# Hybrid convolution and gated-attention block: a different head, and LayerNorm statistics one query block later

## The chip, the cores and the metric

The kernel runs on the eight cores of one Trainium2 chip. Each core computes 4096 of the 32768 tokens by itself, with no exchange between cores. The metric is the device time of the slowest core, in microseconds.

## The reference

x is (16, 2048, 1024) in float32; everything is causal.

```python
h = rms_norm(x, norm_g)
c_val, c_gate, c_z, q, k, v, g_lr, g_r, m_conv, m_gla = split(h @ w_in)
# conv branch
u = c_val * sigmoid(c_gate)
u = depthwise causal conv over 31 positions(u) + conv_b
u = silu(layer_norm(u)) * silu(c_z);   y_conv = u @ w_conv_out
# gated linear attention, 4 heads, key 128, value 256
log_a = log_sigmoid(g_lr @ gate_w2 + gate_b) / 16
S_t = diag(a_t) S_{t-1} + k_t^T v_t;   o_t = q_t S_t / sqrt(128)
y_gla = (rms_norm(o) * silu(g_r)) @ w_gla_out
y = sigmoid(m_conv) * y_conv + sigmoid(m_gla) * y_gla
out = rms_norm(x + y @ w_out, final_g)
```

## The kernel before

A core works through eight tiles of 512 tokens, tile 0 to tile 7. The weights are 88 blocks of 128x1024; a tile uses 96 units (the other eight, the convolution taps, are built in place by L339). Tiles 0 to 2 fetch most blocks in float32 (`sb_stg<-w`, 512 KB each, five staging slots), cast them to bf16 in turn on VectorE (L352) and ScalarE (L355), and a third of them per tile is written back in bf16 (`w_b<-sb_wn`). From tile 3 on all blocks are read back in bf16, with 22 slots. `units()` is called just ahead of the matmuls that use a block; it first casts up to four blocks beyond (`LOOK`), and the casts stand in the engines' queues at that point.

The order of the instructions on each engine is the order in which the program is written; `Sched` only adds the semaphore waits. Every engine takes its own instructions strictly in order, and all hardware DMAs are issued by SyncE (SP) in program order too. Only the 128 KB `gw2` is issued by GpSimd.

**The head.** SP issues the first 128 rows of x (`x0_load(0)`), the constants `cst` (identity, mask, gate weights, taps; 512 KB, in FP slots 0 and 1), the per-channel parameters `pp` (20 KB: 160 bytes in each of 128 rows), the norm gain `Gn` (512 KB, broadcast), the other three row blocks of x, and then the first five weight blocks. VectorE casts five parts of `cst` (L279 to L283), negates four columns of `pp` (L284), and clears `scanm`, `u` and `onesb` (L286 to L290). Then for each of the four row blocks: ScalarE squares x with an accumulated sum (L440), GpSimd makes the reciprocal root by a power with -0.5 read from `pp[:, 26:27]` (L443, L446), VectorE scales (L449), TensorE transposes into the one bank `pb6` (L458), and ScalarE copies to `hT` (L461). The order on ScalarE is square 0, square 1, copy 0, square 2, copy 1, square 3, copy 2, copy 3. The square's elementwise output goes to the `hb` slot (two of them) that L449 then overwrites.

**A tile.** GLU (units 0 to 15), values (16 to 23), convolution (24 to 31), eight query and key blocks (`qk`, h = 0 to 7, L409), the attention's silu gate (`wide_tm`, L645), then the attention with conv-gate and merge-gate blocks between its parts, the two output projections of the branches (L419), and the final projection (L795), among whose work the next tile's norm is prepared.

**The statistics.** After the convolution, the sum over channels and the sum of squares stand in `FP` slots 8 and 9, still spread over 128 partitions. `conv_split(0)` and `conv_split(1)` make a bf16 part and a remainder of each on VectorE (L527, L529), giving four pieces `HP`. `conv_stat` sums them over the partitions by four matmuls with a matrix of ones (L536) into banks 4 and 5. `conv_rstd` makes mean and reciprocal deviation (L541 to L546 on VectorE, L549 and L551 on ScalarE), and `ln(c)` normalises block c (L555 GpSimd, L558 VectorE, L561 ScalarE). VectorE also evicts each query and key block (L663, L667). The order around them:

```python
qk(t, h)
if h == 0: conv_split(1)
if h == 1: conv_stat()
if h == 2: conv_rstd()
if h >= 3: ln(h - 3)
```

The remaining three `ln` calls stand in the first gate half (`wide_tm(t, U_GR(0), ...)`), after each of its first three row blocks. The query and key blocks go to banks 2, 7, 0, 1, 3 in turn.

Of the kernel before, what the change touches and what calls it, by code (L numbers as in the profile page):

```python
# [148 lines left out]
def build_nc(n_tiles=NT):  # L149
# [16 lines left out]
    def newsem(name):  # L166
        dma_sem_names.append(name)
        return name

    with ExitStack() as es:  # L170
        def sb(name, shape, dt):
            return es.enter_context(nc.sbuf_tensor("sb_" + name, shape, dt))
# [55 lines left out]
        def mk(name, n=None):  # L228
            if n is None:
                B[name] = Buf(name)  # L230
            else:
                B[name] = [Buf("%s%d" % (name, i)) for i in range(n)]
# [27 lines left out]
                            d.r[kk] = vv  # L260

        B["cst"] = B["FP"][0]
        mk("taps"); mk("m32")

        def x0_load(s):
            S.op("sp", lambda e: e.dma_start(out=U1[:, 2 * s:2 * s + 2, :].rearrange("p a t -> p (a t)"),
                                             in_=x_d[s * 128:(s + 1) * 128, :]),
                 writes=B["U1"][2 * s:2 * s + 2], dma_sem=newsem("x0_%d" % s))

        x0_load(0)  # L270
        S.op("sp", lambda e: e.dma_start(out=cst, in_=cst_d), writes=[B["FP"][0], B["FP"][1]], dma_sem=newsem("c_cst"))
        S.op("sp", lambda e: e.dma_start(out=pp[:], in_=pp_d), writes=[B["pp"]], dma_sem=newsem("c_pp"))
        S.op("sp", lambda e: e.dma_start(out=Gn[:], in_=ng_d.partition_broadcast(128)), writes=[B["Gn"]],
             dma_sem=newsem("c_gn"))
        for s_ in range(1, 4):
            x0_load(s_)
        S.op("pool", lambda e: e.dma_start(out=gw2[:], in_=gw2_d), writes=[B["gw2"]], dma_sem=newsem("c_gw"))

        S.op("dve", lambda e: e.tensor_copy(out=identb[:], in_=cst[:, 0:128]), reads=[B["cst"]], writes=[B["identb"]])  # L279
# [1 line left out]
        S.op("dve", lambda e: e.tensor_copy(out=wglr[:], in_=cst[:, 256:512]), reads=[B["cst"]], writes=[B["wglr"]])  # L281
        S.op("dve", lambda e: e.tensor_copy(out=taps[:], in_=cst[:, 512:768]), reads=[B["FP"][1]], writes=[B["taps"]])
        S.op("dve", lambda e: e.tensor_copy(out=m32[:], in_=cst[:, 768:800]), reads=[B["FP"][1]], writes=[B["m32"]])  # L283
        S.op("dve", lambda e: e.tensor_scalar(out=pp[:, 32:36], in0=pp[:, 32:36], scalar1=-1.0, scalar2=0.0,  # L284
                                              op0=ALU.mult, op1=ALU.add), reads=[B["pp"]], writes=[B["pp"]])
        S.op("dve", lambda e: e.memset(scanm[:], 1.0), writes=[B["scanm"]])  # L286
        S.op("dve", lambda e: e.memset(scanm[:].rearrange("p (c t) -> p c t", c=4)[:, :, 0:1], 0.0),
             reads=[B["scanm"]], writes=[B["scanm"]])
        S.op("dve", lambda e: e.memset(u[:], 0.0), writes=B["u"])
        S.op("dve", lambda e: e.memset(onesb[:], 1.0), writes=[B["onesb"]])  # L290
# [142 lines left out]
        def pre_elem(t, s):  # L433
            p = s % 2
            if t == 0:
                xs, xbuf = U1[:, 2 * s:2 * s + 2, :].rearrange("p a t -> p (a t)"), B["U1"][2 * s:2 * s + 2]
            else:
                xs, xbuf = xa[:, p, :], [B["xa"][p]]
            col = (t * 4 + s) % 8
            S.op("act", lambda e, p=p, col=col: e.activation(  # L440
                out=hb[:, p, :], in_=xs, func=AF.Square, accum_out=ssx[:, col:col + 1]),
                reads=xbuf, writes=[B["hb"][p], B["ssx"][col]])
# [3 lines left out]
            S.op("pool", lambda e, col=col: e.tensor_tensor(  # L446
                out=ssx[:, col:col + 1], in0=ssx[:, col:col + 1], in1=pp[:, 26:27], op=ALU.pow),
                reads=[B["ssx"][col], B["pp"]], writes=[B["ssx"][col]])
# [323 lines left out]
        def fin(t, s):  # L772
            col = 8 + (t * 4 + s) % 8
            ub = B["U1"][2 * s:2 * s + 2]
            hv = HP[:, 0:2, :].rearrange("p a t -> p (a t)")
            S.op("act", lambda e: e.activation(out=hv, in_=u1v(s), func=AF.Square, accum_out=ssx[:, col:col + 1]),
                 reads=ub, writes=[B["HP"][0], B["HP"][1], B["ssx"][col]])
            S.op("pool", lambda e: e.tensor_scalar(
                out=ssx[:, col:col + 1], in0=ssx[:, col:col + 1], scalar1=1.0 / D, scalar2=EPS,
                op0=ALU.mult, op1=ALU.add), reads=[B["ssx"][col]], writes=[B["ssx"][col]])  # L780
            S.op("pool", lambda e: e.tensor_tensor(
                out=ssx[:, col:col + 1], in0=ssx[:, col:col + 1], in1=pp[:, 26:27], op=ALU.pow),
                reads=[B["ssx"][col], B["pp"]], writes=[B["ssx"][col]])
# [49 lines left out]
        def tile(t):  # L833
# [34 lines left out]
            for h in range(8):  # L868
                qk(t, h)
                if h == 0:  # L870
                    conv_split(1)
                if h == 1:
                    conv_stat()
                if h == 2:
                    conv_rstd()
                if h >= 3:
                    ln(h - 3)
            rbf(t, 0)
            set_pbanks([1, 3, 4, 5, 2, 7, 0])
            wide_tm(t, U_GR(0), sgr, B["sgr"], AF.Silu, False, lambda s: ln(5 + s) if s < 3 else None)  # L880
            wide_tm(t, U_GR(1), sgr, B["sgr"], AF.Silu, False)

            set_pbanks([5, 7])
# [186 lines left out]
```

How the kernel before makes its waits and increments, by code:

```python
    def replay(self, eng, engobj, eng_sems, dma_sems):  # L135
        for o in self.prog[eng]:
            for k, v in o.waits:
                if k[0] == "e":
                    engobj.wait_ge(eng_sems[k[1]], self.cnts[k[1]][v])
                else:
                    engobj.wait_ge(dma_sems[k[1]], v)
            if o.fn is None:
                continue
            inst = o.fn(engobj)
            if o.dma_sem is not None:
                inst.then_inc(dma_sems[o.dma_sem], 16)
            elif o.marked:
                inst.then_inc(eng_sems[eng], 1)
```

## Time and profile before

| | us |
|---|---|
| median of 3 runs | 1612.04 |
| lowest, highest | 1610.75, 1613.39 |
| the profiled execution's own time | 1609.87 |
| span of its slowest core (core 7) | 1608.3 |
| span of its fastest core (core 3) | 1592.6 |
| TensorE busy, core 7 | 1478.3 |

The span is the time from the first to the last instruction of a core; about 1.6 us of the execution lie around it. PE is the matrix engine, PEld its weight loads, DVE VectorE, ACT ScalarE, POOL GpSimd, SP the engine that issues the DMAs. In a timeline the columns are start in us, duration in us, engine, line, operation, output and inputs with shapes, the count, and in brackets the idle time before it and what released it.

### The profile page before, as it was taken

To read this page: it belongs to the slowest core of one execution; us is meant where nothing else is said; L and a number is where in the kernel's file an instruction comes from. 1 tells how busy PE (TensorE), PEld (TensorE's weight loads), DVE (VectorE), ACT (ScalarE), POOL (GpSimd) and SP (SyncE) were. 2 spreads that over 40 slices of the span, in tenths; PEclk is the share of its full clock that TensorE was granted. 3 is DMA by queue.
4 is the path that set the end of the run, shared out by engine and by line. 5 is a ranking of instruction groups with operands and counts; after the bars stand their busy time and mean duration, and the time that the engine had idled before them with its cause. 6 is when DMAs were issued, how large, how long until landed. Compare 5 with 4: busy or idle time off the path is not lost.

```text
span 1608.3 us, 28736 instructions; the slowest of 8 cores (1592.6 to 1608.3 us)
## 1 busy us (share of the span) xinstructions
PE 1478.3 (92%) x8960; PEld 703.2 (44%) x8960; DVE 890.8 (55%) x1259; ACT 705.4 (44%) x1184; POOL 555.2 (35%) x659
## 2 busy tenths in 40 slices
PE   4687989688999899999999999999999999999997
PEld 1233533234544345444554445444544445444553
DVE  3466645475545665476634665376644675366633
ACT  4235755226644256433644245233644246332631
POOL 1123223224223342254423452353423352352512
PEclk9898999889999999999999999999999999999999
DMA  6987899976899868898464955568564856568451
GB/s 184 292 235 222 274 314 318 291 231 200 269 322 286 255 205 252 268 268 243 153 220 143 247 177 184 177 192 242 151 223 145 229 188 200 178 180 241 134 175 53
DMA packets 174820, 352.29 MB, mean 219 GB/s; under 512 B 19536, under 2 KB 60624, under 8 KB 174672
## 3 DMA queue, kind: packets, MB, share of 16 engines
q1 hardware_dynamic: 174528, 350.32, 71.5%
q8 instruction: 76, 1.25, 0.3%
q14 instruction: 72, 0.59, 0.1%
q0 software_dynamic: 144, 0.13, 0.1%
HBM read 301.75 MB, written 48.76 MB: 218 GB/s over the span
## 4 chain that ended last, share of the span: by engine, by line
PE 73%; DMA 10%; DVE 7%; issue 4%; ACT 3%; SPq 2%; POOL 1%; DVEq 0%; POOLq 0%; ACTq 0%
PE ps_pb L409 33%; PE ps_pb L645 13%; PE ps_pb L419 11%; PE ps_pb L795 6%; PE ps_pb L507 4%; DMA sb_stg<-w 4%; DMA usc<-sb_u 3%; DVE sb_U L513 1%; DVE sb_FP L520 1%; SPq L498 1%; DMA w_b<-sb_wn 1%; ACT sb_wn L355 1%; PE ps_pb L707 1%; PE ps_pb L703 1%; PE ps_pb L712 1%
## 5 line engine op out<-in xcount | busy, mean ns | idle before, releaser
L409 PE MATMUL ps_pb<-sb_hT,sb_wn 128*128 128x512 bf16 x2152 | 492.7, 383 | 16.1 <-ACT sb_wn L355 6.9
L409 PEld LDWEIGHTS ps_pb<-sb_hT,sb_wn 128*128 128x128 bf16 x2152 | 209.8, 99 | 271.2 <-issue 38.2
L645 PE MATMUL ps_pb<-sb_wn,sb_hT 128*128 128x512 bf16 x768 | 191.6, 408 | 53.1 <-ACT sb_wn L355 33.1
L409 PE MATMUL ps_pb<-sb_hT,sb_stg 128*128 128x512 bf16 x920 | 207.0, 379 | 1.2 <-issue 0.8
L419 PE MATMUL ps_pb<-sb_big,sb_wn 128*128 128x512 bf16 x744 | 174.7, 382 | 0.4 <-DVE sb_wn L352 0.4
L936 POOL TENSOR_TENSOR sb_yb<-sb_FP 128x512 bf16<-128x512 f32 x64 | 82.7, 1293 | 213.0 <-DVE sb_FP L933 213.0
L645 PEld LDWEIGHTS ps_pb<-sb_wn,sb_hT 128*128 128x128 bf16 x768 | 77.6, 103 | 163.0 <-issue 87.0
L409 PEld LDWEIGHTS ps_pb<-sb_hT,sb_stg 128*128 128x128 bf16 x920 | 89.4, 98 | 105.4 <-issue 2.6
L355 ACT ACTIVATE sb_wn<-sb_stg 128x1024 bf16<-128x1024 f32 x88 | 92.3, 1050 | 98.3 <-DMA sb_stg<-w 98.1
L674 POOL TENSOR_SCALAR sb_Rbf<-sb_Tst,sb_gar 128x256 bf16<-128x256 f32 x128 | 65.7, 531 | 190.8 <-DVE sb_Tst L718 190.7
L522 POOL TENSOR_TENSOR sb_FP<-sb_FP,sb_yb 128x512 f32<-128x512 f32 x56 | 73.8, 1319 | 157.0 <-ACT sb_yb L516 157.0
L555 POOL TENSOR_TENSOR sb_U<-sb_U,sb_FP 128x512 f32<-128x512 f32 x64 | 97.1, 1544 | 57.3 <-DVE sb_FP L541 57.3
L419 PEld LDWEIGHTS ps_pb<-sb_big,sb_wn 128*128 128x128 bf16 x744 | 72.1, 99 | 83.7 <-issue 4.3
L352 DVE CAST sb_wn<-sb_stg 128x1024 bf16<-128x1024 f32 x89 | 68.5, 776 | 63.6 <-DMA sb_stg<-w 63.5
L926 ACT ACTIVATE sb_FP<-ps_pb 128x512 f32<-128x512 f32 x64 | 38.0, 594 | 137.0 <-PE ps_pb L409 116.9
L489 POOL COPY sb_halo<-sb_u 128x30 bf16<-128x30 bf16 x64 | 50.9, 796 | 127.4 <-DVE sb_u L486 127.4
L449 DVE SCALAR_TENSOR_TENSOR sb_hb<-sb_xa,sb_ssx,sb_Gn 128x1024 bf16<-128x1024 f32 x28 | 36.0, 1284 | 102.2 <-POOL sb_ssx L446 102.2
L481 ACT ACTIVATE sb_FP<-ps_pb 128x512 f32<-128x512 f32 x64 | 38.1, 595 | 121.2 <-PE ps_pb L409 80.1
L795 PE MATMUL ps_pb<-sb_wn,sb_yb 128*128 128x512 bf16 x384 | 86.5, 379 | 4.8 <-ACT sb_wn L355 1.8
L740 DVE SCALAR_TENSOR_TENSOR sb_big<-ps_pb,sb_sso,sb_sgr 128x256 bf16<-128x256 f32 x128 | 61.9, 483 | 45.5 <-POOL sb_sso L732 35.5
L507 PE MATMUL ps_pb<-sb_big,sb_wn 128*32 128x512 bf16 x1472 | 80.7, 379 | 2.6 <-issue 2.6
L558 DVE TENSOR_TENSOR sb_U<-sb_U,sb_FP 128x512 f32<-128x512 f32 x64 | 71.1, 1136 | 18.6 <-ACT sb_FP L551 18.6
(115 smaller groups left out, 2083.0 us busy)
## 6 DMA issues: line engine op xcount, KB each, us to landing
sb_stg<-w SPq DMA_DIRECT2D x177, 512.0 KB, 7.7
sb_wn<-w_b SPq DMA_DIRECT2D x329, 256.0 KB, 4.5
sb_stg<-w_b SPq DMA_DIRECT2D x198, 256.0 KB, 3.8
sb_big<-usc SPq DMA_DIRECT2D x256, 135.0 KB, 4.8
w_b<-sb_wn SPq DMA_DIRECT2D x88, 256.0 KB, 6.6
sb_U<-x SPq DMA_DIRECT2D x36, 512.0 KB, 6.6
out<-sb_U SPq DMA_DIRECT2D x32, 512.0 KB, 4.0
sb_xa<-x SPq DMA_DIRECT2D x28, 512.0 KB, 5.4
```

Of the source, the lines that this page charges most:

```text
L352: S.op("dve", lambda e: e.tensor_copy(out=wn[:, slot, :], in_=stg[:, i, :]), reads=[B["stg"][i]], writes=[B["wn"][slot]])
L355: S.op("act", lambda e: e.activation(out=wn[:, slot, :], in_=stg[:, i, :], func=AF.Copy), reads=[B["stg"][i]], writes=[B["wn"][slot]])
L409: S.op("pe", lambda e, bi=bi, kc=kc, wap=wap: e.matmul(pb[bi][:], lhsT=wap[:, kc * 128:(kc + 1) * 128], rhs=hT[:, hbuf, kc, :], start=(kc ...
L419: S.op("pe", lambda e, bi=bi, kc=kc, wap=wap: e.matmul(pb[bi][:], lhsT=wap[:, kc * 128:(kc + 1) * 128], rhs=src[:, kc, :], start=(kc == 0) ...
L507: S.op("pe", lambda e, cbk=cbk, j=j, b=b, c=c, wap=wap: e.matmul(pb[cbk][32 * b:32 * b + 32, :], lhsT=wap[:, b * 256 + j * 32:b * 256 + j ...
L522: S.op("pool", lambda e: e.tensor_tensor(out=FP[:, S2, :], in0=FP[:, S2, :], in1=sq, op=ALU.add), reads=[B["FP"][S2]] + sqbuf, writes=[B[" ...
L555: S.op("pool", lambda e, c=c: e.tensor_tensor(out=U1[:, c, :], in0=U1[:, c, :], in1=FP[:, MU, :], op=ALU.subtract), reads=[B["U1"][c], B[" ...
L558: S.op("dve", lambda e, c=c: e.tensor_tensor(out=U1[:, c, :], in0=U1[:, c, :], in1=FP[:, RS, :], op=ALU.mult), reads=[B["U1"][c], B["FP"][ ...
L645: S.op("pe", lambda e, bi=bi, kc=kc, s=s, wap=wap: e.matmul(pb[bi][:], lhsT=hT[:, hbuf, kc, s * 128:(s + 1) * 128], rhs=wap[:, (kc % 2) * ...
L674: S.op("pool", lambda e, p=p, h=h, s=s: e.tensor_scalar(out=Rbf[:, p, h, :], in0=Tst[:, h, :], scalar1=gar[:, h, s:s + 1], scalar2=1.0, op ...
L795: S.op("pe", lambda e: e.matmul(pb[bi][:], lhsT=yb[:, kc, s * 128:(s + 1) * 128], rhs=wap[:, (kc % 2) * 512:(kc % 2) * 512 + 512], start=( ...
L936: S.op("pool", lambda e, c=c, t1=t1, g2=g2: e.tensor_tensor(out=yb[:, c, :], in0=FP[:, t1, :], in1=FP[:, g2, :], op=ALU.add), reads=[B["FP ...
```

## The change

SP issues `Gn` and the second block of x ahead of `cst`, and `pp` last, after all of x. Four clearings go from VectorE to GpSimd, ahead of the `gw2` transfer that GpSimd issues. A new one-column tile `mh`, set to -0.5 on GpSimd, takes the place of `pp[:, 26:27]` in two powers. The negation of `pp` moves from behind the casts of `cst` to just ahead of the first row block's work; it stays on VectorE. In tile 0 the squares write to `FP` slots 2 and 3. In every tile `conv_stat`, `conv_rstd` and `ln` come one `qk` block later, and the first gate half takes four `ln` calls.

```diff
         x0_load(0)
-        S.op("sp", ... cst ...)
-        S.op("sp", ... pp ...)
         S.op("sp", ... Gn ...)
-        for s_ in range(1, 4):
-            x0_load(s_)
+        x0_load(1)
+        S.op("sp", ... cst ...)
+        x0_load(2)
+        x0_load(3)
+        S.op("sp", ... pp ...)
+        S.op("pool", lambda e: e.memset(mh[:], -0.5), writes=[B["mh"]])
+        S.op("pool", ... memset(scanm, 1.0) ...)
+        S.op("pool", ... memset(scanm every 128th column, 0.0) ...)
+        S.op("pool", ... memset(onesb, 1.0) ...)
+        S.op("pool", ... memset(u, 0.0) ...)
         S.op("pool", ... gw2 dma ...)
         S.op("dve", ... five casts of cst ...)
-        S.op("dve", ... pp[:, 32:36] *= -1.0 ...)
-        S.op("dve", ... the same four memsets ...)
@@ pre_elem
-            S.op("act", ... out=hb[:, p, :], in_=xs, func=AF.Square, accum_out=ssx ...
+            if t == 0:
+                jk, jb = FP[:, 2:4, :].rearrange("p a t -> p (a t)"), B["FP"][2:4]
+            else:
+                jk, jb = hb[:, p, :], [B["hb"][p]]
+            S.op("act", ... out=jk, in_=xs, func=AF.Square, accum_out=ssx ...
@@ pre_elem and fin
-                out=ssx[:, col:col + 1], in0=ssx[:, col:col + 1], in1=pp[:, 26:27], op=ALU.pow),
+                out=ssx[:, col:col + 1], in0=ssx[:, col:col + 1], in1=mh[:], op=ALU.pow),
@@ tile
-                if h == 1:
+                if h == 2:
                     conv_stat()
-                if h == 2:
+                if h == 3:
                     conv_rstd()
-                if h >= 3:
-                    ln(h - 3)
+                if h >= 4:
+                    ln(h - 4)
             rbf(t, 0)
-            wide_tm(t, U_GR(0), ..., lambda s: ln(5 + s) if s < 3 else None)
+            wide_tm(t, U_GR(0), ..., lambda s: ln(4 + s))
@@ after the definitions, ahead of the first loads of w and pre_elem(0, 0)
+        S.op("dve", ... pp[:, 32:36] *= -1.0 ...)
```

## Rows read from the trace of the kernel before

**Rows 1.** The page of core 7: busy time of TensorE, and the chain by engine.
```profile
PE 1478.3 (92%) x8960; PEld 703.2 (44%) x8960; DVE 890.8 (55%) x1259; ACT 705.4 (44%) x1184; POOL 555.2 (35%) x659
...
PE 73%; DMA 10%; DVE 7%; issue 4%; ACT 3%; SPq 2%; POOL 1%; DVEq 0%; POOLq 0%; ACTq 0%
```

**Rows 2.** Windows of core 7: stretch, its length, busy of each engine, clock, DMA share.
```profile
320.00:500.00 180.00, 166.32 (x1003) 77.76 (x1004) 105.12 (x153) 96.41 (x155) 57.61 (x67) 0.93 0.81 257
...
700.00:1608.00 908.00, 885.80 (x5512) 429.68 (x5510) 513.16 (x718) 371.14 (x662) 344.43 (x397) 1.00 0.63 188
```

**Rows 3.** Timeline of TensorE around the statistics of tile 5, then of tile 7.
```profile
1112.06 3.61 PE L409 MATMUL ps_pb<-sb_hT,sb_wn 128*128 128x512 bf16 x16 [0.34 <-ACT sb_yb L516]
...
1115.51 0.38 PE L536 MATMUL ps_pb<-sb_HP,sb_onesb 128*128 128x512 bf16 x1
1117.04 0.38 PE L536 MATMUL ps_pb<-sb_HP,sb_onesb 128*128 128x512 bf16 x1 [0.56 <-DVE sb_HP L527]
1117.84 0.38 PE L536 MATMUL ps_pb<-sb_HP,sb_onesb 128*128 128x512 bf16 x1 [0.42 <-DVE sb_HP L529]
1118.06 1.24 PE L409 MATMUL ps_pb<-sb_hT,sb_wn 128*128 128x512 bf16 x5
...
1480.88 0.38 PE L536 MATMUL ps_pb<-sb_HP,sb_onesb 128*128 128x512 bf16 x1 [0.19 <-DVE sb_HP L527]
...
1483.41 0.38 PE L536 MATMUL ps_pb<-sb_HP,sb_onesb 128*128 128x512 bf16 x1 [0.42 <-DVE sb_HP L529]
1483.63 3.61 PE L409 MATMUL ps_pb<-sb_hT,sb_wn 128*128 128x512 bf16 x16
```

**Rows 4.** Timeline of VectorE and ScalarE in tile 5, same stretch.
```profile
1117.00 0.69 DVE L529 TENSOR_TENSOR sb_HP<-sb_FP,sb_HP 128x512 bf16<-128x512 f32 x1
...
1138.16 0.80 ACT L561 ACTIVATE sb_U<-sb_U,sb_pp 128x512 f32<-128x512 f32 x1
...
1140.82 0.60 ACT L654 ACTIVATE sb_sgr<-ps_pb 128x512 bf16<-128x512 f32 x1 [0.40 <-PE ps_pb L645]
```

**Rows 5.** Timeline of tile 1: statistics, a cast, the gate's matmuls; then one window of TensorE.
```profile
353.04 0.38 PE L536 MATMUL ps_pb<-sb_HP,sb_onesb 128*128 128x512 bf16 x1 [1.84 <-DVE sb_HP L527]
...
355.94 12.67 PE L409 MATMUL ps_pb<-sb_hT,sb_wn 128*128 128x512 bf16 x48
...
375.12 15.44 PE L645 MATMUL ps_pb<-sb_wn,sb_hT 128*128 128x512 bf16 x58 [1.98 <-ACT sb_wn L355]
...
356.00:360.50 4.50, 4.50 (x13) 0.53 0.84 283
```

**Rows 6.** Timeline of the head, core 7.
```profile
11.82 1.87 DVE L289 MEMSET sb_u<- 128x2176 bf16 x1 [0.41 <-DMA sb_Gn<-ng]
...
13.75 1.16 DVE L449 SCALAR_TENSOR_TENSOR sb_hb<-sb_U,sb_ssx,sb_Gn 128x1024 bf16<-128x1024 f32 x1
...
21.96 0.96 POOL L838 MEMSET sb_Tst<- 128x1024 f32 x1
...
23.07 1.90 DVE L352 CAST sb_wn<-sb_stg 128x1024 bf16<-128x1024 f32 x3
...
24.52 1.02 ACT L461 ACTIVATE sb_hT<-ps_pb 128x1024 bf16<-128x1024 bf16 x1 [1.47 <-PE ps_pb L458]
```

**Rows 7.** One line's DMA issues and their landing: `pp`; x blocks 3 and 4; first weight.
```profile
L272 SPq DMA_DIRECT2D sb_pp<-pp x1: 422/422/422, 2.0 to 2.0; - x1
...
DMA to landing us min/median/max: 8.4/8.4/8.4
...
L266 SPq DMA_DIRECT2D sb_U<-x x2: 458/468/478, 3.8 to 4.3; - x2
DMA to landing us min/median/max: 11.1/11.6/12.1
...
L329 SPq DMA_DIRECT2D sb_stg<-w x1: 782/782/782, 4.8 to 4.8; - x1
DMA to landing us min/median/max: 13.4/13.4/13.4
```

More of the change, by code:

```diff
@@ L214, in build_nc @@
         cst = FP[:, 0:2, :].rearrange("p a t -> p (a t)")
+        mh = sb("mh", [128, 1], F32)
         taps = sb("taps", [128, 256], BF16)
@@ L262, in build_nc @@
         B["cst"] = B["FP"][0]
-        mk("taps"); mk("m32")
+        mk("taps"); mk("m32"); mk("mh")
         def x0_load(s):
@@ L270, in build_nc @@
         x0_load(0)
-        S.op("sp", lambda e: e.dma_start(out=cst, in_=cst_d), writes=[B["FP"][0], B["FP"][1]], dma_sem=newsem("c_cst"))
-        S.op("sp", lambda e: e.dma_start(out=pp[:], in_=pp_d), writes=[B["pp"]], dma_sem=newsem("c_pp"))
         S.op("sp", lambda e: e.dma_start(out=Gn[:], in_=ng_d.partition_broadcast(128)), writes=[B["Gn"]],
              dma_sem=newsem("c_gn"))
-        for s_ in range(1, 4):
-            x0_load(s_)
+        x0_load(1)
+        S.op("sp", lambda e: e.dma_start(out=cst, in_=cst_d), writes=[B["FP"][0], B["FP"][1]],
+             dma_sem=newsem("c_cst"))
+        x0_load(2)
+        x0_load(3)
+        S.op("sp", lambda e: e.dma_start(out=pp[:], in_=pp_d), writes=[B["pp"]], dma_sem=newsem("c_pp"))
+        S.op("pool", lambda e: e.memset(mh[:], -0.5), writes=[B["mh"]])
+        S.op("pool", lambda e: e.memset(scanm[:], 1.0), writes=[B["scanm"]])
+        S.op("pool", lambda e: e.memset(scanm[:].rearrange("p (c t) -> p c t", c=4)[:, :, 0:1], 0.0),
+             reads=[B["scanm"]], writes=[B["scanm"]])
+        S.op("pool", lambda e: e.memset(onesb[:], 1.0), writes=[B["onesb"]])
+        S.op("pool", lambda e: e.memset(u[:], 0.0), writes=B["u"])
         S.op("pool", lambda e: e.dma_start(out=gw2[:], in_=gw2_d), writes=[B["gw2"]], dma_sem=newsem("c_gw"))
@@ L283, in build_nc @@
         S.op("dve", lambda e: e.tensor_copy(out=m32[:], in_=cst[:, 768:800]), reads=[B["FP"][1]], writes=[B["m32"]])
[L284 to L290, printed above, removed]
         nar_sems = [newsem("wn%d" % i) for i in range(NX)]
@@ L439, in pre_elem @@
             col = (t * 4 + s) % 8
-            S.op("act", lambda e, p=p, col=col: e.activation(
-                out=hb[:, p, :], in_=xs, func=AF.Square, accum_out=ssx[:, col:col + 1]),
-                reads=xbuf, writes=[B["hb"][p], B["ssx"][col]])
+            if t == 0:
+                jk, jb = FP[:, 2:4, :].rearrange("p a t -> p (a t)"), B["FP"][2:4]
+            else:
+                jk, jb = hb[:, p, :], [B["hb"][p]]
+            S.op("act", lambda e: e.activation(out=jk, in_=xs, func=AF.Square, accum_out=ssx[:, col:col + 1]),
+                reads=xbuf, writes=jb + [B["ssx"][col]])
             S.op("pool", lambda e, col=col: e.tensor_scalar(
@@ L446, in pre_elem @@
             S.op("pool", lambda e, col=col: e.tensor_tensor(
-                out=ssx[:, col:col + 1], in0=ssx[:, col:col + 1], in1=pp[:, 26:27], op=ALU.pow),
-                reads=[B["ssx"][col], B["pp"]], writes=[B["ssx"][col]])
+                out=ssx[:, col:col + 1], in0=ssx[:, col:col + 1], in1=mh[:], op=ALU.pow),
+                reads=[B["ssx"][col], B["mh"]], writes=[B["ssx"][col]])
             S.op("dve", lambda e, p=p, col=col: e.scalar_tensor_tensor(
@@ L781, in fin @@
             S.op("pool", lambda e: e.tensor_tensor(
-                out=ssx[:, col:col + 1], in0=ssx[:, col:col + 1], in1=pp[:, 26:27], op=ALU.pow),
-                reads=[B["ssx"][col], B["pp"]], writes=[B["ssx"][col]])
+                out=ssx[:, col:col + 1], in0=ssx[:, col:col + 1], in1=mh[:], op=ALU.pow),
+                reads=[B["ssx"][col], B["mh"]], writes=[B["ssx"][col]])
         def fin_b(t, s):
@@ L871, in tile @@
                     conv_split(1)
-                if h == 1:
+                if h == 2:
                     conv_stat()
-                if h == 2:
+                if h == 3:
                     conv_rstd()
-                if h >= 3:
-                    ln(h - 3)
+                if h >= 4:
+                    ln(h - 4)
             rbf(t, 0)
             set_pbanks([1, 3, 4, 5, 2, 7, 0])
-            wide_tm(t, U_GR(0), sgr, B["sgr"], AF.Silu, False, lambda s: ln(5 + s) if s < 3 else None)
+            wide_tm(t, U_GR(0), sgr, B["sgr"], AF.Silu, False, lambda s: ln(4 + s))
             wide_tm(t, U_GR(1), sgr, B["sgr"], AF.Silu, False)
@@ L955, in tile @@
             wout(t, more)
-        pos["load"] = 0
+        S.op("dve", lambda e: e.tensor_scalar(out=pp[:, 32:36], in0=pp[:, 32:36], scalar1=-1.0, scalar2=0.0,
+                                              op0=ALU.mult, op1=ALU.add), reads=[B["pp"]], writes=[B["pp"]])
         while load_one(pos["load"], 0):
```

## The prediction

> **What bounds the kernel now.** I read the page first. On core 7 TensorE is busy for 1478.3 us, 92% of the span, and makes 73% of the chain that ended last; DMA has 10% [rows 1]. The windows split this in two. From 700 us on (tiles 3 to 7) TensorE is busy in 885.8 of 908 us at full clock, with the DMA engines at 63%: the end is set by TensorE alone, and an idle microsecond of TensorE taken away there is a microsecond off the time, unless something else becomes late. In tile 1 it is busy in 166.3 of 180 us, the clock averages 0.93 and DMA is at 81% [rows 2]: there the weights' fetches and casts share the limit. I then read the timelines at the two places that the change touches, the head and the statistics. The sum below is made against the profiled execution, 1609.87 us (span 1608.3 and 1.6 around it); the median of the runs is 1612.04, 2.2 more, and I carry the difference in time over to it.
>
> **Part 1, statistics one block later, tiles 3 to 7.** In tile 5 query blocks 0 and 1 take TensorE from 1112.06, at 0.216 us a matmul (sixteen: 3.46), to the first L536 at 1115.51. The next block starts at 1118.06. Four matmuls cost 4 x 0.216 = 0.86, so 2.55 - 0.86 = 1.69 us are idle, because VectorE makes the four pieces later than TensorE wants them: the last piece (L529) runs from 1117.00 to 1117.69, and its matmul starts at 1117.84 [rows 3, 4]. In tile 7 the stretch from 1480.88 to 1483.63 is 2.75, with 0.19 idle before it, so 2.08 is lost [rows 3]. The five tiles show 2.54, 2.35, 2.55, 2.55 and 2.94 in order (tiles 5 and 7 are shown), in all 12.93 - 5 x 0.86 = 8.6 us.
>
> With query block 2 put ahead, TensorE comes to the four matmuls 8 x 0.216 = 1.73 later, and to the last of them at 1115.51 + 1.73 + 0.65 = 1117.89, when its piece is ready to start at 1117.84. Nothing paces the pieces from behind: VectorE's queue ahead of them holds only the eviction of block 0, long finished. In tile 7 the same sum gives 1483.07 against 1483.41, so 0.3 remains. Gain: 8.6 - 0.3 = 8.3 us. The number of instructions does not change.
>
> What is late next? In absolute time the sums in banks 4 and 5 end where they did (near 1118.3), so L541 is ready no later; it now stands behind the eviction of block 3 in place of block 2, some 0.3 us later at most, since both blocks come 1.7 earlier. All `ln` work therefore keeps its absolute place within half a microsecond, while TensorE runs 1.7 ahead of it. Its last ScalarE piece ends at 1138.96, and by 1140.82 ScalarE waits for TensorE again when it evicts the gate (L654) [rows 4]; seven banks serve the gate, so TensorE has several blocks of 1.73 before it needs one back. That cover is about 5 us against 1.7 used. If it were gone, each tile would lose what it gained; this is a rival below. Banks 4 and 5 are needed again only by the third row block of the gate. Bounds of the part: -10 (each tile as tile 7) to 0, taken -8.3.
>
> **Part 2, the same in tiles 0 to 2.** Here the stall is longer: in tile 1 1.84 idle before the first L536, then 2.90 to the next block at 355.94, less 0.86: 3.9 us. Only 1.73 of it can be filled by one block. Later in the same tile TensorE waits for a ScalarE cast of a weight block until 375.12, 1.98 idle [rows 5]. Would that wait take the gain? The cast stands in ScalarE's queue behind `ln` pieces. As `ln` moves back by one block and the casts do not, each cast gets one `ln` step less ahead of it, 1.3 to 1.7 us (as these steps follow each other), while the `ln` chain is at most 0.3 later. So in tiles 1 and 2 some 1.3 should pass, in tile 0 less, as the stretch after it runs on fetches. I take 3.5 for the three tiles together; bounds 0 (all taken by fetches, as the 81% of DMA in tile 1 allows) and 8 (three full blocks of 1.73, and the clock, see below).
>
> Right after this stall in tile 1 the granted clock averages 0.53 over 356.0 to 360.5, that is mostly the lower level, 1.2 GHz; thirteen matmuls take 4.5 us where at 0.216 they would take 2.8, so 1.7 is lost to the clock [rows 5]. A busier TensorE might keep it. The Trainium skill (TensorE: Matmul & The Clock Gate, "What's actually happening") says that the gate follows how busy the engine has been, and the trace agrees in that 0.53 stands behind 4.7 us in which it mostly waited. By that rule alone tiles 0 and 1 would give some 3 us more; this changes no term of the sum.
>
> **Part 3, the head.** Before, the first scaling L449 starts at 13.75 and the last copy to `hT` at 24.52, 10.77 later. What holds L449 to 13.75 is VectorE's own clearing: `u` alone is 11.82 to 13.69 [rows 6]. That goes to GpSimd. The nearest row for it there is a clearing of 128x1024 in 0.96 us [rows 6], so 2176 columns take 2.0, and all five clearings 3; doubled, 6. GpSimd has nothing to do before the first square is done (about 9 us), and the `gw2` transfer behind the clearings is needed only after the last copy. Cost nothing; if the cover were gone, at most the 3 us. Removing the clearing would let L449 start about 2 us earlier.
>
> But the negation of `pp` stays on VectorE, still ahead of the first L449, and `pp` is now issued last. Before, it is issued at 2.0 and lands 8.4 later, at 10.4. The last block of x, issued at 4.3, lands at 16.4, and the first weight block, issued at 4.8, at 18.2: transfers land in the order of issue, about 1.6 us apart [rows 7]. `pp` now stands between these two, with the same bytes ahead of it. I take 17.3, between 15.4 (x, no longer behind `pp`, lands a microsecond earlier and `pp` with it) and 18.2. Every VectorE instruction of the four row blocks is behind that wait. The Trainium skill (DMA: Bandwidth & Descriptors, "Queues, rings and completion order") says that each DMA engine consumes descriptors in ring order; it speaks against this order of issue, and the trace agrees, with 10.4, 16.4 and 18.2 in the order of issue.
>
> L449 then starts at 17.3 + 0.2 = 17.5 in place of 13.75, +3.75. From there the chain is the old one: ScalarE's order is unchanged, so copy 0, square 2, copy 1, square 3, the GpSimd power and L449 follow as before. The earlier second block of x saves 0.25 once. The scratch target of the squares gives nothing: squares 2 and 3 wait for ScalarE's own copies ahead of them, not for the `hb` slots. Last copy at 28.0, +3.5 us. The first weight casts stand behind the last L449 (23.07, rows 6), so the first freed staging slots and all further fetches shift too; DMA had finished the first five fetches and was idle, and catches up nothing. Head: +3.5, bounds +1.7 and +4.5.
>
> **The sum.** +3.5 - 8.3 - 3.5 = -8.3 us: 1601.6 for the profiled execution, 1603.7 for the median.
>
> **The rivals.**
> *A: the early tiles give nothing.* Fetches hold tiles 0 to 2 (DMA at 81% in tile 1 [rows 2]) and take back part 2. Against it, the waits named there end on casts that move forward. +3.5 - 8.3 = -4.8: 1607.2.
> *B: the head is not delayed.* If 20 KB slip past the large transfers, L449 goes by `cst` and starts before 13.75; head about -1. For it, `pp` moved few bytes; against it, the order of landings [rows 7]. -1 - 8.3 - 3.5 = -12.8: 1599.2.
> *C: the clock is kept in tiles 0 and 1*, giving the 1.7 of each on top: 3.4 more, 1600.3.
> *D: the stall comes back inside the tile, slower.* TensorE, 1.7 ahead, waits for a bank whose eviction stands behind `ln` pieces on ScalarE or VectorE. It decides once `ln` ends more than some 3 us later against TensorE. Then parts 1 and 2 are zero and the head remains: +3.5, 1615.5. The change would then not do what it says. Against it, ScalarE is back to waiting at 1140.82 [rows 4].
> *E: `pp` lands behind all five staged weights*, +10 in the head with -8.3 and no part 2: 1613.7.
>
> **Chances.** Forecast 0.46, A 0.20, B 0.10, C 0.12, D 0.08, E 0.04. The predicted time is that of the forecast. The range from 1598.5 to 1610 takes in the bounds of the head (+1.7 to +4.5), of part 2 (0 to -8) and most of A, B and C. A measurement of this kernel tells from no change what differs by over 0.2%, 3.2 us. A falls partly inside that, D and part of E are slower: faster 0.82, same 0.11, slower 0.07.
>
> **What would show it.** In the tile timelines the four L536 follow at 0.22 us, and the next block starts 0.9 after the first. The window of the last five tiles shortens by about 8 us. In the head L284's successor waits for `pp` until about 17.3, the first L449 starts near 17.5 and the last copy near 28. The prediction is wrong if the first L449 starts before 14, if L536 still has idle time of over 0.5 in a late tile, or if new idle time of TensorE shows at the gate or the first attention part.

## The result, and the profile after

The changed kernel takes 1596.83 us (median of 20 runs) against 1612.34 us, a ratio of 0.9901 with a 95% interval from 0.9874 to 0.9928: 16 us faster. In some executions of either kernel the cores of one die run at a lower granted clock and the time is longer, up to 1836 us; the ratio compares the others. The forecast was 8.3 us; the gain is nearly twice that, and the time lies below the range, which ended at 1598.5. The profiled execution took 1596.76 us; its slowest core is now core 1, with a span of 1595.2 us against 1608.3, and the mean span of the eight cores fell from 1603.5 to 1586.1 us.

The page of core 1, the same two views as [rows 1], then the two windows that answer to [rows 2]:

```profile
PE 1475.5 (92%) x8960; PEld 704.1 (44%) x8960; DVE 892.4 (56%) x1255; ACT 704.3 (44%) x1184; POOL 559.3 (35%) x664
...
PE 73%; DMA 10%; DVE 6%; issue 4%; ACT 4%; SPq 3%; POOL 1%; DVEq 0%; POOLq 0%; ACTq 0%
```

```profile
320.00:500.00 180.00, 169.27 (x1036) 80.11 (x1037) 111.22 (x157) 97.57 (x158) 62.36 (x72) 0.96 0.85 264
...
700.00:1608.00 908.00, 878.84 (x5491) 427.92 (x5489) 511.33 (x715) 369.72 (x661) 339.36 (x395) 1.00 0.63 187
```

The page hardly tells the two kernels apart. The windows say a little more: between 320 and 500 us TensorE issues 1036 matmuls where it issued 1003, and its clock averages 0.96 where it averaged 0.93. But core 1 is here compared with core 7. In the mean of all eight cores the same window has 1042 matmuls against 1024 and a clock of 0.97 against 0.95, so about half of the difference is one of cores.

The statistics in tile 5 and in tile 7 of core 1, TensorE's timeline, answering to [rows 3]:

```profile
1105.68 3.83 PE L410 MATMUL ps_pb<-sb_hT,sb_wn 128*128 128x512 bf16 x17
1109.35 1.03 PE L540 MATMUL ps_pb<-sb_HP,sb_onesb 128*128 128x512 bf16 x4
1110.24 2.97 PE L410 MATMUL ps_pb<-sb_hT,sb_wn 128*128 128x512 bf16 x13
...
1471.10 1.27 PE L540 MATMUL ps_pb<-sb_HP,sb_onesb 128*128 128x512 bf16 x4
1472.21 2.97 PE L410 MATMUL ps_pb<-sb_hT,sb_wn 128*128 128x512 bf16 x13
```

The four matmuls with ones are now one unbroken group, from 1109.35 to the next block at 1110.24, 0.89 us where [rows 3] has 2.55. In tile 7 it is 1.11 where it was 2.75 and 0.19 of idle time before. ScalarE catches up with the gate as before:

```profile
1130.36 0.80 ACT L565 ACTIVATE sb_U<-sb_U,sb_pp 128x512 f32<-128x512 f32 x1
...
1133.00 0.60 ACT L658 ACTIVATE sb_sgr<-ps_pb 128x512 bf16<-128x512 f32 x1 [0.38 <-PE ps_pb L649]
```

The head, core 1, answering to [rows 6], and the landing of `pp` there and on core 7 [rows 7]:

```profile
1.91 1.92 POOL L285 MEMSET sb_u<- 128x2176 bf16 x1
...
15.25 0.17 DVE L961 TENSOR_SCALAR sb_pp<-sb_pp 128x4 f32<-128x4 f32 x1 [3.29 <-DMA sb_pp<-pp]
15.49 2.48 DVE L453 SCALAR_TENSOR_TENSOR sb_hb<-sb_U,sb_ssx,sb_Gn 128x1024 bf16<-128x1024 f32 x2
...
26.17 1.02 ACT L465 ACTIVATE sb_hT<-ps_pb 128x1024 bf16<-128x1024 bf16 x1 [1.25 <-PE ps_pb L462]
```

```profile
L279 SPq DMA_DIRECT2D sb_pp<-pp x1: 558/558/558, 4.4 to 4.4; - x1
...
DMA to landing us min/median/max: 10.8/10.8/10.8
...
L279 SPq DMA_DIRECT2D sb_pp<-pp x1: 1066/1066/1066, 5.2 to 5.2; - x1
DMA to landing us min/median/max: 11.6/11.6/11.6
```

VectorE stands idle for 3.29 us until `pp` is there, and the first scaling follows at once. Between it and the last copy lie 10.68 us. On core 7 `pp` lands at 16.8 and the last copy starts at 27.81, against 24.52 before.

For a sum by stage, one core is not enough, since tiles 0 to 2 differ from core to core by several microseconds. The table has means over the eight cores of one profiled execution each, read from where TensorE starts the low-rank gate matmuls of each tile (L584, L588 after). "Head" is the first of these; each tile ends at the next. The last column is the mean of tiles 3 to 6.

| kernel | head | end of tile 0 | of tile 1 | of tile 2 | a late tile | mean span |
|---|---|---|---|---|---|---|
| before | 25.2 | 247.8 | 467.9 | 669.4 | 182.6 | 1603.5 |
| after | 27.9 | 242.5 | 459.3 | 660.5 | 181.0 | 1586.1 |

So the head costs 2.7, tiles 0 to 2 give 8.0 + 3.3 + 0.3 = 11.6, and tiles 3 to 7 the other 8.5 of the 17.4 by which the mean span fell. Head and late tiles are close to the forecast (3.5 and 8.3). The early tiles were forecast at 3.5. The same table's numbers for the kernels of the experiments stand there.

One profiled execution is a rough measure of the early tiles. The kernel before had a mean span of 1603.5 us in its profiled execution, but 1599.5 to 1600.4 in the mean of the executions with which the experiments' ratios were formed. The 11.6 may be too large by as much as this; the timed ratios below decide.

### The profile page after: what moved, and what is told of

Read it like the earlier page. It is cut to its first block, busy times and chain, and to the rows that moved or that the text cites. A ratio compares the mean times of both kernels' runs of the same rounds, so it can differ in the third digit from the quotient of the medians.

```text
span 1595.2 us, 28748 instructions; the slowest of 8 cores (1576.5 to 1595.2 us)
## 1 busy us (share of the span) xinstructions
PE 1475.5 (92%) x8960; PEld 704.1 (44%) x8960; DVE 892.4 (56%) x1255; ACT 704.3 (44%) x1184; POOL 559.3 (35%) x664
## 4 chain that ended last, share of the span: by engine, by line
PE 73%; DMA 10%; DVE 6%; issue 4%; ACT 4%; SPq 3%; POOL 1%; DVEq 0%; POOLq 0%; ACTq 0%
PE ps_pb L410 32%; PE ps_pb L649 13%; PE ps_pb L420 11%; PE ps_pb L799 6%; DMA sb_stg<-w 4%; PE ps_pb L511 4%; DMA usc<-sb_u 3%; DVE sb_U L517 2%; SPq L502 1%; DVE sb_FP L524 1%; ACT sb_wn L356 1%; PE ps_pb L462 1%; PE ps_pb L707 1%; PE ps_pb L716 1%; PE ps_pb L711 1%
## 5 line engine op out<-in xcount | busy, mean ns | idle before, releaser
L649 PE MATMUL ps_pb<-sb_wn,sb_hT 128*128 128x512 bf16 x768 | 195.3, 413 | 53.9 <-ACT sb_wn L356 37.7
L649 PEld LDWEIGHTS ps_pb<-sb_wn,sb_hT 128*128 128x128 bf16 x768 | 78.7, 104 | 166.2 <-issue 92.3
L526 POOL TENSOR_TENSOR sb_FP<-sb_FP,sb_yb 128x512 f32<-128x512 f32 x56 | 73.9, 1320 | 160.2 <-ACT sb_yb L520 160.0
L562 DVE TENSOR_TENSOR sb_U<-sb_U,sb_FP 128x512 f32<-128x512 f32 x64 | 74.4, 1197 | 17.2 <-ACT sb_FP L555 17.2
```

What stands on the lines that cost most here:

```text
L526: S.op("pool", lambda e: e.tensor_tensor(out=FP[:, S2, :], in0=FP[:, S2, :], in1=sq, op=ALU.add), reads=[B["FP"][S2]] + sqbuf, writes=[B[" ...
L649: S.op("pe", lambda e, bi=bi, kc=kc, s=s, wap=wap: e.matmul(pb[bi][:], lhsT=hT[:, hbuf, kc, s * 128:(s + 1) * 128], rhs=wap[:, (kc % 2) * ...
```

## Experiments

Each was timed in five rounds beside the kernel before, where nothing else is said. The theories: **F**, the early gain is TensorE's idle time at the statistics filled by a query block, with the clock that it keeps; **Q**, a good part is queue order, that is, the casts of the gate's weights stand one LayerNorm step earlier on ScalarE and VectorE; and a rival, that the early gain came from the **head** or was spread between executions. The first expectations call F and Q together theory 1 and the head theory 2.

### The changed kernel again

No edit.

> The changed kernel unaltered, for comparison on one chip. Expected ratio to before 0.990 (0.987 to 0.993), about 15 us faster. Mean over the eight cores of the traces so far: head +2.7 us, tiles 0 to 2 -11.6 us, tiles 3 to 7 -8.5 us. Theory 1 (the gain of tiles 0 to 2 comes from the statistics shift, mostly from casts that stand one LayerNorm step earlier in the queues) and theory 2 (part of it is the head, whose delay is taken back by the fetch-bound first tile) agree here.

Ratio 0.9896 (0.9880 to 0.9911). Stage means 28.1, 243.2, 456.1, 658.3, late tile 181.0. Against the first profile of the same kernel the ends of tiles 0 to 2 differ by 0.7 to 3.2 us: that is the grain of these stage means, and the early gain is well above it.

### The changed head alone

```diff
-                if h == 2:
+                if h == 1:
                     conv_stat()
-                if h == 3:
+                if h == 2:
                     conv_rstd()
-                if h >= 4:
-                    ln(h - 4)
+                if h >= 3:
+                    ln(h - 3)
```

> The changed head with the statistics in their old place. By my prediction's rule, that the head's delay passes to the end in full: +2.7 to +3.5 us, 1615 us. Theory 2, the fetch-bound first tile absorbs the delay before its statistics: +0 us or even a gain, 1609 to 1613, the last copy to hT still 2.7 us later on the mean of the cores while the statistics of tile 0 start no later than before (119.5 us).

Ratio 1.0011 (0.9974 to 1.0048). The head ends at 28.2 on the mean, 3.0 later than before. Tile 0 ends at 248.5 (+0.7) and tile 1 at 467.4 (-0.5). (Tile 2 ends at 674.4, since cores 2 and 3 had a clock of 0.85 in it; the other six end it at 668.6, against 671.0 before.) So the head brings no gain: the rival falls. How much of its delay reaches the end this run does not settle: the interval goes from -4 to +8 us. In its five executions under 1614 us the mean span of the cores is 1601.9, against 1600.4 before, or +1.5 with an uncertainty of some 2.3.

### Statistics shifted in tiles 3 to 7 alone, and in tiles 0 to 2 alone

```diff
             conv_split(0)
+            lt = 1 if t >= 3 else 0
             for h in range(8):
-                if h == 1:
+                if h == 1 + lt:
                     conv_stat()
-                if h == 2:
+                if h == 2 + lt:
                     conv_rstd()
-                if h >= 3:
-                    ln(h - 3)
+                if h >= 3 + lt:
+                    ln(h - 3 - lt)
-            wide_tm(... lambda s: ln(5 + s) if s < 3 else None)
+            wide_tm(... lambda s: ln(5 - lt + s) if s < 3 + lt else None)
```

The other kernel has `1 if t < 3 else 0`. Both have the old head.

> The old head; the statistics shifted in tiles 3 to 7 alone. All theories: -8.3 us (1604 us), each of these five tiles 1.6 to 2.0 us shorter in the mean of the cores, tiles 0 to 2 as before. If it is only -4 or less, the late tiles do not carry their part.

> The old head; the statistics shifted in tiles 0 to 2 alone. Prediction's part 2: -3.5 us. Theory 1: -8 to -11 us (1602 to 1604), of it 4 to 5 us between the statistics and the end of tile 0. Theory 2: -3 to -5 us here and the rest in the head-only kernel. A third possibility, that the gain of the early tiles is the spread of their fetches from one execution to the next, would leave the stage times of the cores scattered by more than the difference.

Late tiles: 0.9948 (0.9935 to 0.9962), or 1610.59 x 0.0052 = 8.4 us; a late tile takes 180.9 in place of 182.6, and tiles 0 to 2 end as before (247.3, 465.7, 667.4). Early tiles: 0.9924 (0.9910 to 0.9937), 12.2 us; tile 2 ends at 656.0, the late tiles are unchanged at 182.6. The early tiles alone give a little more than the 8 to 11 us of theory 1, and three and a half times my 3.5. The product of the two ratios is 0.9872 against 0.9896 for the whole change: some 4 us are left for the head's cost, with about 4 of uncertainty.

### The two halves of the shift, in all tiles, old head

`stat_moved_ln_kept`, then `ln_moved_stat_kept`:

```diff
-                if h == 1:
+                if h == 2:
                     conv_stat()
```

```diff
-                if h >= 3:
-                    ln(h - 3)
+                if h >= 4:
+                    ln(h - 4)
-            wide_tm(... lambda s: ln(5 + s) if s < 3 else None)
+            wide_tm(... lambda s: ln(4 + s))
```

> Old head; in every tile the four matmuls with ones come one query block later, but the mean and deviation follow them at once and the LayerNorm steps keep their old places against the weight casts. Theory F (filling: all of the gain is TensorE's idle time filled by the block, with the clock it keeps): the full -20 us of the two halves together (ratio 0.987), early tiles -12. Theory Q (queue order: part of the early gain is that the casts of the gate's weights stand one LayerNorm step earlier): the late tiles still give -8, the early tiles only -6 to -8, ratio 0.990 to 0.992; the stretch from the gate's first matmul to the attention in tile 0 stays near 22.2 us instead of 20.0.

> Old head; the statistics and deviation in their old places, only the LayerNorm steps one block later. Theory F: no gain anywhere, ratio 1.000, since TensorE's wait at the statistics stays. Theory Q: tiles 3 to 7 unchanged, tiles 0 to 2 gain 3 to 5 us, ratio 0.997 to 0.998; the stretch from the gate's first matmul to the attention in tile 0 falls from 22.2 towards 20 us.

Only the matmuls moved: 0.9916 (0.9891 to 0.9940), 13.5 us; head 24.9, tile 2 ends at 657.5, a late tile takes 181.0. Only the LayerNorm steps moved: 0.9921 (0.9900 to 0.9943), 12.7 us; head 25.4, tile 2 ends at 654.6, a late tile is unchanged at 182.6. In the late tiles F holds alone. In the early tiles it is not enough: with the matmuls moved F had expected a ratio of 0.987, outside the interval, and Q 0.990 to 0.992, which was met. Q's own part was expected at 3 to 5 us with the LayerNorm steps moved, and the 12.7 are about three times that.

What the moved matmuls alone give in tiles 0 to 2 is not well fixed. By the ratios it is 13.5 less the 8.4 of the late tiles, 5.1 us with an uncertainty of about 4.6; the stage means of the one profiled execution say 12 against the kernel before and 10 against the kernel with the shift in the late tiles alone. That execution took 1591.46 us, where the median was 1595.05, so it is one of the shortest of six.

TensorE's idle time, summed over tiles 0 to 2, mean of the eight cores of one execution each, shows what either half acts on. The first two columns count gaps of over 0.15 us before the instructions of L536 and of L645 (L540 and L649 after), the third all of the time in which TensorE is not busy. The number of matmuls is the same, so "busy" falls where they run at the higher clock.

| | before the statistics matmuls | before the gate's matmuls | all idle | busy |
|---|---|---|---|---|
| before | 8.1 | 13.6 | 83.0 | 561.2 |
| matmuls moved | 3.9 | 13.3 | 75.3 | 557.3 |
| LayerNorm moved | 8.1 | 6.0 | 73.0 | 556.1 |
| after (first profile) | 4.0 | 10.5 | 73.6 | 559.0 |
| after (second profile) | 4.0 | 10.8 | 73.9 | 556.4 |

The waits of TensorE in tile 0, core 7, from 110 to 162 us, those at the two places: who waited for whom, total, times, longest. Before, then with the matmuls moved, then with the LayerNorm steps moved.

```profile
PE ps_pb L645 <- ACT sb_wn L355: 5.1, 2, 2.6
PE ps_pb L536 <- DVE sb_HP L527: 2.9, 2, 1.8
PE ps_pb L645 <- DVE sb_wn L352: 1.1, 2, 0.6
```

```profile
PE ps_pb L645 <- ACT sb_wn L355: 4.9, 2, 2.5
PE ps_pb L536 <- DVE sb_HP L527: 1.2, 1, 1.2
```

```profile
PE ps_pb L536 <- DVE sb_HP L527: 2.9, 2, 1.8
PE ps_pb L645 <- ACT sb_wn L355: 1.9, 2, 1.3
```

The wait at the statistics (L536) falls only where the matmuls moved, the wait of the gate (L645) for the cast only where LayerNorm moved. The timelines show how. ScalarE (ACT) and the gate's matmuls in tile 0, core 7, before:

```profile
137.45 0.81 ACT L561 ACTIVATE sb_U<-sb_U,sb_pp 128x512 f32<-128x512 f32 x1
139.19 0.81 ACT L561 ACTIVATE sb_U<-sb_U,sb_pp 128x512 f32<-128x512 f32 x1 [0.93 <-DVE sb_U L558]
139.91 1.04 ACT L355 ACTIVATE sb_wn<-sb_stg 128x1024 bf16<-128x1024 f32 x1
140.86 0.80 ACT L561 ACTIVATE sb_U<-sb_U,sb_pp 128x512 f32<-128x512 f32 x1
...
143.87 0.81 ACT L561 ACTIVATE sb_U<-sb_U,sb_pp 128x512 f32<-128x512 f32 x1 [2.21 <-DVE sb_U L558]
144.59 1.04 ACT L355 ACTIVATE sb_wn<-sb_stg 128x1024 bf16<-128x1024 f32 x1
...
145.77 4.59 PE L645 MATMUL ps_pb<-sb_wn,sb_hT 128*128 128x512 bf16 x14 [2.51 <-ACT sb_wn L355]
```

and with the LayerNorm steps moved:

```profile
133.28 0.82 ACT L561 ACTIVATE sb_U<-sb_U,sb_pp 128x512 f32<-128x512 f32 x1
134.00 1.04 ACT L355 ACTIVATE sb_wn<-sb_stg 128x1024 bf16<-128x1024 f32 x1
...
134.95 1.51 ACT L561 ACTIVATE sb_U<-sb_U,sb_pp 128x512 f32<-128x512 f32 x2
...
136.36 1.04 ACT L355 ACTIVATE sb_wn<-sb_stg 128x1024 bf16<-128x1024 f32 x1
...
137.54 12.68 PE L645 MATMUL ps_pb<-sb_wn,sb_hT 128*128 128x512 bf16 x58 [1.34 <-ACT sb_wn L355]
```

Before, two LayerNorm steps stand ahead of the first of these casts and four ahead of the second, and a step is slow because it waits for VectorE (0.93 and 2.21 idle), whose own queue holds casts too. With LayerNorm moved, one and three stand ahead. The last matmul of the gate that has to wait starts 3.4 us after the first of these LayerNorm pieces has ended, not 7.5.

Two stretches of the tiles, means over the eight cores: from the first statistics matmul to the gate's first (with one query block, 1.7 us, fewer in it where the statistics are later), and from there to the attention's first.

| | tile 0 | tile 1 | tile 2 |
|---|---|---|---|
| before | 16.4, 22.2 | 15.0, 21.1 | 13.1, 17.0 |
| matmuls moved | 13.6, 22.1 | 12.8, 21.1 | 9.9, 18.6 |
| LayerNorm moved | 15.7, 16.2 | 14.0, 17.3 | 13.3, 15.7 |
| after (first profile) | 13.0, 20.0 | 12.2, 20.2 | 9.9, 19.1 |

The second stretch falls by 6.0, 3.8 and 1.3 with LayerNorm moved, but only by 2.2, 0.9 and -2.1 in the full change. The halves do not add: in the full change the idle time at the gate falls by 3 us, not by 7.6. The deviation also moves one block back in the full change, so the whole LayerNorm chain stands later against TensorE, and the gate again waits for casts behind it. That reason is argued from the order of the queues; the numbers of the two tables are what is shown.

The clock: over the first stretch and the 3.5 us ahead of it, the granted clock averages 0.86 in tile 0 and 0.91 in tile 1 before, 0.94 and 0.95 after (0.96 and 0.99 in the second execution). In these stretches TensorE runs less at the 1.2 GHz level where it waits less.

### The wait for `pp`

```diff
-        S.op("dve", ... pp[:, 32:36] *= -1.0 ...)        # ahead of the loads and scalings
         ...
         pre_pe(0, 3)
+        S.op("dve", ... pp[:, 32:36] *= -1.0 ...)
```

> The changed kernel with one instruction moved: the negation of pp stands behind the four row blocks' scalings instead of ahead of them, so that no scaling waits for pp. My prediction's account of the head (all behind the landing of pp): the first scaling starts near 13 us (after the casts of cst, which land at 11 to 12.5) instead of 15.5 to 17.1, the last copy to hT ends 3.5 to 4 us earlier than in the changed kernel, near 22.5 to 23.5 at its start. Time: -3 to -4 us against the changed kernel (ratio to before 0.987) if the head passes to the end; no change (0.990) if the fetch-bound first tile absorbs it.

Ratio 0.9879 (0.9854 to 0.9904). The head ends at 24.7 on the mean, 3.4 earlier than in the changed kernel on its second profile, tile 0 at 238.3 (-4.9) and tile 2 at 653.4 (-4.9); the mean span is 1579.4 against 1584.1. Core 7:

```profile
12.21 2.48 DVE L453 SCALAR_TENSOR_TENSOR sb_hb<-sb_U,sb_ssx,sb_Gn 128x1024 bf16<-128x1024 f32 x2
...
21.43 0.17 DVE L968 TENSOR_SCALAR sb_pp<-sb_pp 128x4 f32<-128x4 f32 x1
22.88 1.02 ACT L465 ACTIVATE sb_hT<-ps_pb 128x1024 bf16<-128x1024 bf16 x1 [1.25 <-PE ps_pb L462]
```

The first scaling starts at 12.21 in place of 17.14 on that core, behind the casts of `cst`, and the last copy is as much earlier. The account of the head holds. By the ratios the gain over the changed kernel is 2.7 us, which their intervals do not tell from none. The mean span of the cores over the executions of the ratio fell by 19.0 where it fell by 16.3 with the changed kernel, again 2.7, with an uncertainty of as much. So most of the head's time seems to pass to the end; it is not shown to pass in full.

### The scratch for the squares

```diff
-            if t == 0:
+            if t < 0:
                 jk, jb = FP[:, 2:4, :]...
```

> The changed kernel with the squares of the first tile written to hb as before. By the prediction's part 3 the scratch target gives nothing, since ScalarE's own copies stand ahead of squares 2 and 3: the first scaling and the last copy to hT lie 10.7 us apart, as in the changed kernel (15.49 to 26.17 on core 1). If the scratch matters, the distance grows by 1 us or more.

One execution alone, 1593.8 us. On core 7 the first scaling starts at 16.10 and the last copy at 26.77, 10.67 apart, and so they are with the scratch (17.14 and 27.81); on the other cores they are 10.67 to 10.68 apart. The scratch gives nothing in the head.

### Two blocks later

```diff
-                if h == 2:
+                if h == 3:
                     conv_stat()
-                if h == 3:
+                if h == 4:
                     conv_rstd()
-                if h >= 4:
-                    ln(h - 4)
+                if h >= 5:
+                    ln(h - 5)
-            wide_tm(t, U_GR(0), ..., lambda s: ln(4 + s))
-            wide_tm(t, U_GR(1), ..., False)
+            wide_tm(t, U_GR(0), ..., lambda s: ln(3 + s))
+            wide_tm(t, U_GR(1), ..., False, lambda s: ln(7) if s == 0 else None)
```

The first kernel, `two_later`, has the same order but leaves out `ln(7)`, the normalisation of the last channel block.

> The changed kernel with the statistics, deviation and LayerNorm two query blocks later than before instead of one. In tiles 3 to 7 no wait is left to fill: +-0 against the changed kernel. In tiles 0 and 1, where 3.9 to 4.4 us were idle and one block fills 1.7, a second block fills up to 1.7 more each: -2 to -4 us (ratio 0.988) by the filling theory; if LayerNorm now ends too late for the gate's evictions, tiles 3 to 7 lose time at the gate or the attention, +2 or more each.

> The changed kernel with statistics, deviation and LayerNorm two query blocks later, and all eight LayerNorm steps in place (the kernel two_later left out the last one, ln(7), and measured 0.985 so). Both theories of the early tiles: tile 0 from its first statistics matmul to the gate near 8.7 us and the gate to the attention near 21, the end of tile 2 at 653 to 655 us of the cores' mean with the head at 28. If the missing step made its time, it falls back to 0.989.

Without `ln(7)` 0.9854 (0.9834 to 0.9874); complete, 0.9867 (0.9848 to 0.9886), between the 0.985 and the 0.989 of the expectation. Tile 2 ends at 652.1 and 654.1, against 658.3 in the changed kernel with the same head. In tile 0 the first stretch is 8.7: two blocks (3.5) are gone from it, and 4.2 of waiting and of lower clock (0.86 before, 1.00 here). A late tile takes 180.9, so nothing was left to fill there, and nothing was lost by LayerNorm ending later.

### A version that beats both

Built on the changed kernel: `pre_elem(0, 0)` stands ahead of the five casts of `cst`, the negation of `pp` behind `pre_pe(0, 3)`, and the order in the tiles is

```diff
                 if h == 2:
                     conv_stat()
                 if h == 3:
                     conv_rstd()
-                if h >= 4:
-                    ln(h - 4)
+                if h >= 5:
+                    ln(h - 5)
-            wide_tm(t, U_GR(0), ..., lambda s: ln(4 + s))
-            wide_tm(t, U_GR(1), ..., False)
+            wide_tm(t, U_GR(0), ..., lambda s: ln(3 + s))
+            wide_tm(t, U_GR(1), ..., False, lambda s: ln(7) if s == 0 else None)
```

> A version to beat both: the changed head with the casts of cst behind the first scaling and the negation of pp behind all four, so that the first transposes start as soon as the identity is cast; statistics one block later, LayerNorm steps two blocks later than before. Expected from the parts: head's last copy starts near 20 to 21 us (against 26.2 to 27.8 in the changed kernel), -6 us; late tiles as in the changed kernel; early tiles a further -3 to -5 us from the casts that stand another step earlier. Together -9 to -11 against the changed kernel, ratio to before 0.983 to 0.985. If the head is absorbed by the fetch-bound tile 0, only -3 to -5 (0.987).

1577.82 us against 1611.89, ratio 0.9804 (0.9781 to 0.9826): 32 us faster than before and some 15 faster than the change. The expectation (0.983 to 0.985) was too small again. Head 22.8, tile ends 233.1, 443.3 and 639.8, mean span 1565.8. The stretch from the gate to the attention is 16.8, 16.9 and 13.8 us, and the first stretch 13.0, 11.8 and 9.9: the waits at the statistics and at the gate now both fall. Against the changed kernel's second profile the head gives 5.3 us and tiles 0 to 2 give 13.2, where 3 to 5 had been expected. The last copy of the head starts at 22.15 on core 1, not at 20 to 21: the first scaling starts at 9.95, but the transposes wait for the identity, cast at 12.54 when `cst` has landed:

```profile
9.95 1.28 DVE L448 SCALAR_TENSOR_TENSOR sb_hb<-sb_U,sb_ssx,sb_Gn 128x1024 bf16<-128x1024 f32 x1 [9.95 <-POOL sb_ssx L445]
...
12.54 0.23 DVE L959 CAST sb_identb<-sb_FP 128x128 bf16<-128x128 f32 x1 [1.30 <-DMA sb_FP<-cst]
...
22.15 1.02 ACT L460 ACTIVATE sb_hT<-ps_pb 128x1024 bf16<-128x1024 bf16 x1 [1.25 <-PE ps_pb L457]
```

## Why the prediction was wrong, point by point

**Part 1, tiles 3 to 7: right.** -8.3 was forecast; -8.4 was measured with the shift in these tiles alone, and -8.5 in the stage means. The remainder in tile 7 showed too (1.11 against 0.86 without a wait). The cover held: 180.9 to 181.0 us a tile in every kernel with the matmuls moved by one or two blocks, and rival D is gone.

**Part 3, the head: right in its mechanism, a little large.** +3.5 on core 7 was forecast from `pp` landing at 17.3; it landed at 16.8, and the last copy came 3.3 later. On the mean of the cores it is +2.7. That it passes to the end in full, as the sum took it, is not shown: +1.5 and 2.7 were seen, each with an uncertainty of over 2. Rival B (`pp` slips past) and E (behind the staged weights) did not happen. The Trainium skill (DMA: Bandwidth & Descriptors, "Queues, rings and completion order") has each DMA engine take its descriptors in ring order. The trace agrees: 20 KB issued at 4.4 to 5.2 took 10.8 to 11.6 us behind the large transfers, where 8.4 had been enough from 2.0.

**Part 2, tiles 0 to 2: the step that failed.** I wrote "some 1.3 should pass, in tile 0 less" and took 3.5 with bounds 0 and 8; the shift there alone measured 12.2. The account of the statistics was nearly right in itself: TensorE's idle time before the four matmuls fell from 8.1 to 4.0 us over the three tiles, close to the 3.5 that I took for the whole part. What failed is what I added to it and took from it: three sizes were wrong.

First, the moved casts. I used them only as the reason why the filled time would pass, at one LayerNorm step of 1.3 to 1.7 us each, and gave them no gain of their own. They cost TensorE more than that, because a cast on ScalarE stands behind LayerNorm steps which in turn wait for VectorE: moved alone, the LayerNorm steps give 12.7 us, and the idle time at the gate falls from 13.6 to 6.0. In the full change it falls by 3.

Second, the fetches. "Fetches hold tiles 0 to 2" (rival A, and my "in tile 0 less") was read from a DMA share of 81%, an average over a tile. Around the statistics, over the first stretch and the 3.5 us ahead of it, the share is only 0.53 in tile 0 and 0.50 in tile 1, as the mean of the cores. With the change it is 0.78 and 0.65 there in its first profile: the fetches had room to move up with the rest, and the 12.2 show that they took back little.

Third, the clock, rival C, which the sum left out. TensorE's busy time in tiles 0 to 2, for the same matmuls, fell from 561.2 to 559.0 in one execution and to 556.4 in the other, or 2 to 5 us. All of its idle time fell by 9, so the waits are the larger part; some 2 us of these 9 lie neither at the statistics nor at the gate, and no run says where they come from. How the 12.2 us divide between fill and queue order is not settled either, since the halves do not add.

The upper bound of 8 for part 2 was built from the block and the clock alone and left out the queue order that the same paragraph had named. With 8 and the head at 3.5 the sum is 1599.2, with the head at its bound of 1.7 it is 1597.4; so the bounds of the sum did not reach 1596.8.

## What to carry to other kernels

When an instruction group is moved in program order, count every other instruction that it changes places with on each in-order queue; here the LayerNorm steps, moved alone behind one more weight cast, gave 12.7 us, nearly as much as the moved matmuls gave in all eight tiles (13.5). Two halves of a move need not add. Read a resource's share in the very stretch of the change, not over the tile. A small transfer on which an early instruction of an in-order engine waits should not be issued behind large ones, and its consumer should stand where it is needed.

## What the runs showed of the hardware

- Moving 20 KB (`pp`) from the third to the seventh issue made its landing 6.4 us later on core 7 (10.4 to 16.8). No run varied its size.
- Clearing 128x2176 bf16 takes 1.92 us on GpSimd (above) and 1.87 on VectorE [rows 6]: no difference that matters.
- The same bf16 cast of 128x512 on VectorE (L531 in tile 0, core 1, after) takes 1.31 us while a GpSimd addition runs (from 121.42 for 1.47 us) and 0.42 us when GpSimd is idle. The slow one ends 0.28 us after the addition, and so it does in the kernel before (121.48 and 121.20, core 7). It is the first link of the chain that the statistics wait for.

```profile
121.42 1.47 POOL L526 TENSOR_TENSOR sb_FP<-sb_FP,sb_yb 128x512 f32<-128x512 f32 x1 [0.20 <-ACT sb_yb L520]
...
121.86 1.31 DVE L531 CAST sb_HP<-sb_FP 128x512 bf16<-128x512 f32 x1
...
125.09 0.42 DVE L531 CAST sb_HP<-sb_FP 128x512 bf16<-128x512 f32 x1
```

- The average clock around the statistics in tiles 0 and 1 rose from 0.86 and 0.91 to 0.94 and 0.95 with less waiting there. The Trainium skill (TensorE: Matmul & The Clock Gate, "What's actually happening") has the gate follow how busy the engine has been; these four numbers agree.
- This program spreads by 1 to 3 us from execution to execution in the fetch-heavy tiles even in the mean of all cores (0.7, 3.2 and 2.2 at the ends of tiles 0 to 2 in two executions of the changed kernel), while the mean of a TensorE-bound tile repeats to 0.1 us (182.6 in four profiles, 180.9 to 181.1 in nine). An effect of 3 us in the first kind needs the timed ratio; in the second a single profile shows it.
